# Relative bias products moved behind the sums of the first norm, in the place of its filler products

## The chip, the cores and the metric

The program runs on one core of a Trainium2 chip. A core has engines that work side by side, each through its own list of instructions in order: TensorE (PE, matrix products; its weight loads are shown as PEld), VectorE (DVE), ScalarE (ACT), GpSimd (POOL) and SyncE (SP, which here only starts transfers). They wait for each other through semaphores. The metric is the device time of one execution in microseconds (us); less is better. Before the change it is 2672.57 us, the median of three runs (2672.18 to 2675.38).

## The reference, cut to what matters

The program is four layers of transformer-like blocks on 512 tokens with 1024 features. The first thing that it computes, and the only one whose order changes, is the modulated norm ahead of the first mixer:

```python
def rms_norm(x, gain):
    xf = x.astype(jnp.float32)
    y = xf * lax.rsqrt(jnp.mean(xf * xf, axis=-1, keepdims=True) + EPS)
    return (y * gain.astype(jnp.float32)).astype(x.dtype)

def modulation(c, w, b):
    return jnp.split(jax.nn.silu(c) @ w + b, 3, axis=-1)

def sandwich(x, mod, g_pre, g_post, fn):
    shift, scale, gate = mod
    h = rms_norm(x, g_pre) * (1.0 + scale[:, None]) + shift[:, None]
    return x + gate[:, None] * rms_norm(fn(h), g_post)
```

The products that are moved have nothing to do with that norm. They prepare the attention of the second layer, several hundred microseconds later: a table of biases by distance, one row for each of 24 heads.

```python
    bias = bias_table[t5_bucket(jnp.maximum(dist, 0) * dil)].astype(jnp.float32).transpose(2, 0, 1)
    ...
    s = jnp.einsum('brnqhe,brnkhe->brnhqk', qs, kk) + bias
```

## The kernel before, in words

Features lie on the 128 partitions in 8 chunks (`x[:, c, :]`, 128 by 512 tokens). Weights come in units of 1 MB through a buffer of two slots (`raw`); ACT copies a unit into a rounded high part `whi` (`split`), POOL subtracts to get the low part `wlo`, and each product of a layer is three matmuls (high by high, low by high, high by low; lines 774 to 776). The order on every engine is written out by hand: each engine has a program of its own, which calls helpers one after the other.

The start of the program is this, with the names that the change touches:

- SP starts the transfers of `vecs`, `cst`, `x`, the first weight unit, eight units of modulation weights (`adw_a`, `adw_b`), the second weight unit and more. ACT starts those of `onehot` and `relb`.
- `bias_rows` (PE, line 1289): for each of three groups one product of `relb` (33 rows, 8 columns) with 384 columns of `onehot`, into the first three banks `LB[0]` to `LB[2]`.
- `write_bias` (ACT, line 2250): copies the three banks to `biasr`, and starts three transfers (line 2254) of 12 KB to a scratch tensor in memory, which the second layer reads back. `biasr` lies in the same memory as `hhi`, the output of the first norm. So nothing of `hhi` may be written until these transfers have landed (semaphore `scr_out`, 48 for all three).
- `load_root` (ACT, line 1953): loads the table of the square root, and `squares` (line 1933) squares the 8 chunks of `x`. PE sums each over the partitions (`feature_sum`, line 898).
- `keep_busy(3, LB[3])` (PE, line 906): three products of 128 by 128 with 256 columns, whose result nobody reads.
- `root` (ACT, line 1950) takes the square root of the sums, DVE the reciprocal (line 2711), and `root_rows` (PE, line 923) spreads it over the partitions.
- `first_rows(p)` (PE, line 1023) multiplies the modulation weights of two chunks, ACT copies them out (line 1999), `first_columns(p)` (PE, line 1031) turns them into columns, DVE makes scale and shift (lines 2840 to 2844) and scales two chunks of `x` (line 2720), ACT writes `hhi` (line 2012), DVE `hlo` (line 2750), and then PE can do the first layer's products for these chunks. This goes round four times, for p from 0 to 3.

A matmul on 4-byte floats is two instructions on PE in the trace, so the three products of `bias_rows` are six there.

Of the kernel before, what the change touches and what calls it, by code (L numbers as in the profile page):

```python
# [44 lines left out]
BIAS_PITCH = 384  # L45
# [156 lines left out]
def program(nc, a, out, stop):  # L202

    with ExitStack() as ctx:
        base = [(nc.sbuf_base + 63) // 64 * 64]

        def sb(name, shape, dt=F32, at=None):

            size = int(np.prod(shape[1:])) * 4
            off = base[0] if at is None else at  # L210
            if at is None:
                base[0] = (off + size + 31) // 32 * 32
            return nc.alloc_sbuf_tensor_at(name, shape, dt, offset=off)
# [45 lines left out]
        def vec(name, i=0, n=1):  # L259
            at, _ = VEC[name]  # L260
            return vecs[:, at + i:at + i + n]
# [40 lines left out]
        onehot = sb("onehot", [P, 3 * BIAS_PITCH], F32, h_at)  # L302
        relb = sb("relb", [P, 24], F32, h_at + 4608)
# [62 lines left out]
        s = Semaphores()  # L366
# [153 lines left out]
        LB = [ctx.enter_context(nc.psum_tensor(f"lin{i}", [P, T], F32)) for i in range(4)]  # L520
# [46 lines left out]
        for _, kc, nc_ in PLAN:  # L567
            offs.append(offs[-1] + P * kc * nc_)
# [108 lines left out]
        def _(pool):  # L677
# [64 lines left out]
            if stop > 4:  # L742
                hy_out = [kind for kind, _, _ in plan].index("hy_out")
                lows(0, hy_out + 1)
                gated_inputs()
                recurrent_branch()
                lows(hy_out + 1, len(plan))
            else:
                lows(0, len(plan))
# [3 lines left out]
        def _(pe):  # L753
# [72 lines left out]
            def lin(units, xs, chunks=None, after=None, held=None, there=0):  # L826

                _, kc, w = plan[st.u]
                first = None if chunks is None else (chunks, n.at(chunks) - there)
                for j in range(units):  # L830
                    fm_unit(st.u % 2, st.tile, kc, w // P, xs, first if j == 0 else None,
                            None if after is None else (lambda t, j=j: after(j * (w // P) + t)), None,
                            held if j == 0 else None)
                    st.u += 1
                    st.tile += w // P
                if chunks is not None:
                    n.up(chunks, kc - there)
# [64 lines left out]
            def keep_busy(rounds, bank=None):  # L902

                spare_bank = LB[(st.tile + 2) % 4] if bank is None else bank
                for _ in range(rounds):
                    pe.matmul(spare_bank[:, 0:2 * P], ident, cst[:, 0:2 * P], start=True, stop=True)

            def feature_sum(k):

                pe.wait_ge(s.sq_ok, n.up(s.sq_ok))  # L910
                chunk_sums(B4, sq[:, k % 2, :], k == 0, k == DC - 1).then_inc(s.ss_mm, 1)
# [15 lines left out]
            def root_rows(after=0):  # L927

                keep_busy(1 if after else 0)
                pe.wait_ge(s.rr_ok, n.up(s.rr_ok))  # L930
                spread_rows(B7, r_rows[:, :]).then_inc(s.rr_mm, 1)
                keep_busy(after)
# [80 lines left out]
            def first_rows(p):  # L1013

                bank = B4 if p else B5
                if p > 1:
                    pe.wait_ge(s.nb_ok, 2 * p - 1)
                for half in range(2):
                    k = FIRST_ADA[2 * p + half]
                    pe.wait_ge(ada_first_in[k], 16)  # L1020
                    for c in range(DC):
                        b = 32 * (c % 4)
                        mm = pe.matmul(bank[b:b + 32, 256 * half:256 * half + 256], silu_c[:, c:c + 1].broadcast_to([P, 32]),
                                       ada_first[k][:, c * 256:(c + 1) * 256], start=(c < 4), stop=(c >= 4))
                    mm.then_inc(s.rows_mm, 1)

            def first_columns(p):

                pe.wait_ge(s.ada_acc, n.up(s.ada_acc))
                for i in range(4):  # L1030
                    mm = pe.matmul((B4 if p else B5)[:, i:i + 1], tmp[:, p % 2, i * P:(i + 1) * P], one_per_row,
                                   start=True, stop=True)
                mm.then_inc(s.ada_mm, 1)

            def first_sums():

                for c in range(DC):
                    feature_sum(c)
                keep_busy(3, LB[3])
                root_rows()  # L1040
                first_rows(0)
                first_columns(0)

            def hgrn_mixer():
# [236 lines left out]
                    sums_after(t)  # L1281
                lin(3, hidden, None, lambda t: sums_after(t + 2))
                root_rows(2)

            def bias_rows():

                pe.wait_ge(s.extra_in, 32)
                for g in range(3):
                    pe.matmul(LB[g][0:8, 0:BIAS_PITCH], relb[0:33, 8 * g:8 * g + 8],
                              onehot[0:33, g * BIAS_PITCH:(g + 1) * BIAS_PITCH], start=True, stop=True)\  # L1290
                        .then_inc(s.bias_mm, 1)

            def attention(steps, banks, S, PT, before, between, group=1, fill=None):

# [572 lines left out]

            pe.wait_ge(s.ready, 1)
            pe.wait_ge(s.ones_in, 16)
            bias_rows()  # L1870
            pe.wait_ge(s.silu_ok, 1)
            first_sums()
            pe.wait_ge(s.bias_ok, 3)
            hgrn_mixer()
# [18 lines left out]
        def _(act):  # L1893
# [3 lines left out]
            def split(slot, size):  # L1897

                act.wait_ge(s_raw[slot], n.up(s_raw[slot], 16))
                act.activation(whi[:, slot, 0:size], raw[:, slot, 0:size], ACT.Copy).then_inc(s.whi_ok, 1)  # L1900
# [51 lines left out]
            def load_root():  # L1952
                act.activation(spare, eps_rms, ACT.Sqrt)
# [41 lines left out]
            def first_norm():  # L1995

                def rows_out(p):
                    act.wait_ge(s.rows_mm, 2 * p + 2)
                    act.activation(tmp[:, p % 2, :], (B4 if p else B5)[:, :], ACT.Copy).then_inc(s.ada_acc, 1)

                rows_out(0)
                for p in range(4):
                    shifted_chunk(0, 2 * p)
                    shifted_chunk(0, 2 * p + 1)
                    if p < 3:
                        rows_out(p + 1)
                    if p == 2:
                        split(1, UNIT)

            def shifted_chunk(ls, c):  # L2010
                    act.wait_ge(s.nb_ok, n.up(s.nb_ok))
                    act.activation(hhi[:, c, :], (B5, B6)[c % 2][:, :], ACT.Identity, bias=mods[:, ls, c:c + 1])\
                        .then_inc(s.hi_ok, 1)
# [232 lines left out]
            def write_bias():  # L2246

                for g in range(3):
                    act.wait_ge(s.bias_mm, g + 1)
                    act.activation(biasr[0:8, g, :], LB[g][0:8, 0:BIAS_PITCH], ACT.Copy, scale=BIAS_SCALE)\  # L2250
                        .then_inc(s.bias_ok, 1)
                act.wait_ge(s.bias_ok, 3)
                for g in range(3):
                    act.dma_start(scratch.ap()[g], biasr[0:8, g, :]).then_inc(s.scr_out, 16)
# [409 lines left out]
            act.wait_ge(s.c_in, 16)  # L2664
            act.wait_ge(s.ready, 1)
            act.activation(silu_c, vec("c", 0, 8), ACT.Silu).then_inc(s.silu_ok, 1)
            write_bias()
            load_root()
            act.wait_ge(s.x_in, 16)
            squares(lambda c: x[:, c, :])  # L2670
            root(1.0 / D, eps_rms)
            split(0, UNIT)
            act.wait_ge(s.scr_out, 48)
            first_norm()
            hgrn_mixer()
            if stop > 1:
# [1058 lines left out]
```

## Time and profile before

| | |
|---|---|
| median of 3 runs | 2672.57 us (2672.18 to 2675.38) |
| the profiled execution's own time | 2679.25 us |
| its span, first to last instruction | 2677.5 us |
| PE busy | 2619.9 us, 98% of the span |
| DVE, ACT, POOL busy | 44%, 36%, 36% |
| mean granted clock of TensorE | 0.994 |

All times in rows are in microseconds from the start of the span, if not marked ns. A row of the timeline has the start, the time until the last instruction of the row ends, the engine, the line of the kernel, the operation, what it writes and reads, the shape and the number of instructions; in brackets, how long the engine was idle ahead of it and what it waited for. A row of windows has the busy time of each engine in one stretch, and the granted clock of TensorE (1.00 is 2.4 GHz, 0.50 is 1.2 GHz). The first change of the granted clock that this trace holds is at 20.7 us; in stretches before that the column reads 1.00 without a record behind it.

### The profile page before, as it was taken

Reading aid. Unit: us, or ns where it says so; the run is one execution under the profiler, and the core shown is the slowest. Engines: PE = TensorE matmul, PEld = TensorE weight load, DVE = VectorE, ACT = ScalarE, POOL = GpSimd, SP = SyncE. Lnnn points to the kernel's source line nnn. Section 1 sums busy time; section 2 is a strip of 40 time slices with the busy share of each in tenths; the row PEclk is TensorE's granted clock in tenths of the full one; section 3 lists DMA queues with packets and bytes.
Section 4 is the critical chain, followed back from the end, with each engine's and each line's share of the span. In section 5 each row is a group of like instructions: output and inputs, shape, how many; then the busy total and the mean of one; then the engine's idle time right before and its main releaser. Section 6 shows DMA issues by size and latency. Waiting matters only on the chain.

```text
span 2677.5 us, 36238 instructions
## 1 busy us (share of the span) xinstructions
PE 2619.9 (98%) x14164; PEld 2116.0 (79%) x14164; DVE 1186.8 (44%) x1984; ACT 968.3 (36%) x1399; POOL 961.7 (36%) x257
## 2 busy tenths in 40 slices
PE   8999999999999999999999999999998999999998
PEld 6887787888777777888877678888877778888887
DVE  4566543343523235101258853715424565361542
ACT  4354522212533334222244843212234774321222
POOL 2222343444232223444333734444442213444442
PEclk9999999999999999999999999999999999999999
DMA  8532244542222212232222022222321112222221
GB/s 323 190 135 82 107 159 148 196 166 101 90 71 71 71 64 79 86 102 94 84 91 93 17 87 94 94 94 97 105 88 53 44 48 71 98 104 96 94 94 63
DMA packets 44032, 270.93 MB, mean 101 GB/s; under 512 B 4943, under 2 KB 8679, under 8 KB 15752
## 3 DMA queue, kind: packets, MB, share of 16 engines
q1 hardware_dynamic: 39888, 265.71, 28.2%
q10 hardware_dynamic: 4024, 3.54, 0.6%
q8 instruction: 86, 1.41, 0.2%
q14 instruction: 34, 0.28, 0.0%
HBM read 267.09 MB, written 2.13 MB: 101 GB/s over the span
## 4 chain that ended last, share of the span: by engine, by line
PE 70%; issue 22%; POOL 5%; DVE 2%; ACT 1%; POOLq 0%; ACTq 0%; DVEq 0%
PE lin L774 20%; PE lin L776 20%; PE lin L775 20%; POOL wlo L691 5%; PE lin L1322 2%; PE bank L1306 1%; PE bank L1340 1%; PE bank L1487 1%; PE bank L923 0%; PE lin L1326 0%; PE bank L1479 0%; PE lin L1479 0%; PE bank L1720 0%; PE bank L898 0%; DVE lr L3389 0%
## 5 line engine op out<-in xcount | busy, mean ns | idle before, releaser
L691 POOL TENSOR_TENSOR wlo<-raw,whi 128x2048 fp32r<-128x2048 f32 (+3 forms) x212 | 918.2, 4331 | 1671.3 <-ACT whi L1900 1671.3
L774 PE MATMUL lin<-hhi,whi 128*128 128x512 f32 x1960 | 778.2, 397 | 9.5 <-POOL wlo L691 3.6
L776 PE MATMUL lin<-hhi,wlo 128*128 128x512 f32 x1960 | 766.1, 391 | 0.0
L775 PE MATMUL lin<-hlo,whi 128*128 128x512 f32 x1960 | 765.7, 391 | 0.0
L1900 ACT ACTIVATE whi<-raw 128x2048 fp32r<-128x2048 f32 (+3 forms) x212 | 383.2, 1807 | 930.8 <-PE lin L776 863.6
L774 PEld LDWEIGHTS lin<-hhi,whi 128*128 128x128 f32 x1960 | 369.4, 188 | 102.0 <-issue 15.2
L774 PE MATMUL lin<-ghi,whi 128*128 128x512 f32 x1136 | 446.3, 393 | 3.6 <-POOL wlo L691 2.8
L776 PE MATMUL lin<-ghi,wlo 128*128 128x512 f32 x1136 | 442.8, 390 | 0.0
L775 PE MATMUL lin<-glo,whi 128*128 128x512 f32 x1136 | 442.5, 390 | 0.0
L776 PEld LDWEIGHTS lin<-hhi,wlo 128*128 128x128 f32 x1960 | 369.4, 188 | 78.4
L775 PEld LDWEIGHTS lin<-hlo,whi 128*128 128x128 f32 x1960 | 369.7, 189 | 75.4 <-issue 1.4
L774 PEld LDWEIGHTS lin<-ghi,whi 128*128 128x128 f32 x1136 | 213.7, 188 | 49.2 <-issue 4.8
L776 PEld LDWEIGHTS lin<-ghi,wlo 128*128 128x128 f32 x1136 | 213.5, 188 | 44.6
L775 PEld LDWEIGHTS lin<-glo,whi 128*128 128x128 f32 x1136 | 213.7, 188 | 43.9 <-issue 0.2
L3485 DVE TENSOR_TENSOR sq<-tmp 128x512 f32<-128x512 f32 x64 | 174.1, 2721 | 112.1 <-ACT tmp L2644 112.1
L3042 DVE TENSOR_TENSOR sq<-tmp,lin 128x512 f32<-128x512 f32 x40 | 27.5, 687 | 338.9 <-PE lin L776 320.6
L2048 ACT ACTIVATE tmp<-lin 128x512 f32<-128x512 f32 x40 | 23.9, 598 | 155.3 <-PE lin L776 155.3
L2644 ACT ACTIVATE tmp<-lin 128x512 f32<-128x512 f32 x64 | 37.6, 588 | 98.7 <-PE lin L776 98.7
L2825 DVE SCALAR_TENSOR_TENSOR bank<-adw_a,small,bank 128x256 f32<-128x256 f32 x144 | 70.5, 490 | 5.1
L3496 DVE TENSOR_TENSOR m<-m,lin 128x512 f32<-128x512 f32 x16 | 11.0, 687 | 137.2 <-PE lin L776 137.2
L3135 DVE TENSOR_REDUCE small<-lin 128x1 f32<-128x128 f32 (+3 forms) x96 | 46.7, 487 | 46.5 <-PE lin L1326 45.6
L3275 DVE TENSOR_TENSOR m<-m,lin 128x512 f32<-128x512 f32 x16 | 11.0, 687 | 118.7 <-PE lin L776 118.7
(476 smaller groups left out, 2734.1 us busy)
## 6 DMA issues: line engine op xcount, KB each, us to landing
raw<-in_w SPq DMA_DIRECT2D x171, 1024.0 KB, 4.9
adw_a<-in_ada SPq DMA_DIRECT2D x30, 1024.0 KB, 5.1
adw_b<-in_ada SPq DMA_DIRECT2D x18, 1024.0 KB, 6.8
raw<-in_w SPq DMA_DIRECT2D x20, 768.0 KB, 4.2
raw<-in_w SPq DMA_DIRECT2D x16, 640.0 KB, 3.9
raw<-in_w SPq DMA_DIRECT2D x5, 512.0 KB, 3.5
x<-in_x SPq DMA_DIRECT2D x1, 2048.0 KB, 9.9
out<-x SPq DMA_DIRECT2D x8, 256.0 KB, 2.1
```

The lines of the kernel that those rows point to most:

```text
L691: nc.gpsimd.tensor_tensor(wlo[:, slot, 0:size], raw[:, slot, 0:size], whi[:, slot, 0:size].bitcast(F32), ALU.subtract).then_inc(s.wlo_ok, 1)
L774: pe.matmul(dst, lh, rh, start=first, stop=False)
L775: pe.matmul(dst, lh, rl, start=False, stop=False)
L776: return pe.matmul(dst, ll, rh, start=False, stop=last)
L1306: pe.matmul(bank[0:64, at], p.pick[b], PT[(u - 1) % 4][:, b, :], start=(b == 0), stop=(b == q.j))
L1322: pe.matmul(bank[:, 0:q.w], q.q, q.k, start=True, stop=False)
L1900: act.activation(whi[:, slot, 0:size], raw[:, slot, 0:size], ACT.Copy).then_inc(s.whi_ok, 1)
L2644: act.activation(tmp[:, t, :], LB[(t0 + 2 * j + t) % 4][:, :], ACT.Relu).then_inc(s.ev_a, 1)
L2825: ins = v.scalar_tensor_tensor(acc[:, k % 2, :] if last else b, slot[:, c * 256:c * 256 + 256], silu_c[:, c:c + 1], b, ALU.mult, ALU.add)
L3042: v.tensor_tensor(sq[:, j, :], tmp[:, j, :], LB[(t0 + 2 * j + 1) % 4][:, :], ALU.mult)\
L3135: ins = v.tensor_reduce(top, banks[i % len(banks)][:, 0:q.w], AX_X, ALU.max, negate=True)
L3485: v.tensor_tensor(sq[:, t % 2, :], tmp[:, t % 2, :], tmp[:, t % 2, :], ALU.mult)\
```

## The change

Three edits. On PE, `bias_rows` no longer stands at the very start; it stands behind the sums of the first norm, where the three filler products were, and those are gone. On ACT, `write_bias` (three copies and three starts of transfers) moves from ahead of `load_root` to behind the split of the first weight unit. The wait for `scr_out` moves with it: it stood ahead of `first_norm`, and now stands inside it, behind the copy of the first modulation rows and ahead of the first write of `hhi`.

```diff
             def first_sums():

                 for c in range(DC):
                     feature_sum(c)
-                keep_busy(3, LB[3])
+                bias_rows()
                 root_rows()
                 first_rows(0)
                 first_columns(0)
...
             pe.wait_ge(s.ready, 1)
             pe.wait_ge(s.ones_in, 16)
-            bias_rows()
             pe.wait_ge(s.silu_ok, 1)
             first_sums()
             pe.wait_ge(s.bias_ok, 3)
...
                 rows_out(0)
+                act.wait_ge(s.scr_out, 48)
                 for p in range(4):
                     shifted_chunk(0, 2 * p)
                     shifted_chunk(0, 2 * p + 1)
...
             act.activation(silu_c, vec("c", 0, 8), ACT.Silu).then_inc(s.silu_ok, 1)
-            write_bias()
             load_root()
             act.wait_ge(s.x_in, 16)
             squares(lambda c: x[:, c, :])
             root(1.0 / D, eps_rms)
             split(0, UNIT)
-            act.wait_ge(s.scr_out, 48)
+            write_bias()
             first_norm()
```

The function `bias_rows` itself is unchanged; it only stands higher in the file, so that lines between shift.

PE, the start of its program (what is marked - stood there before, what is marked + stands there now; a row is one matmul of the source, two instructions in the trace):

```order
 L752 UNCONDITIONAL_BRANCH
-L1289 MATMUL lin<-onehot,relb 8x384 x3
 L898 MATMUL bank<-sq,cst 32x128 x32
-L906 MATMUL lin<-cst 128x256 x3
+L1039 MATMUL lin<-onehot,relb 8x384 x3
 L923 MATMUL bank<-r_rows,cst 128x128 x4
 L1023 MATMUL bank<-adw_a_132,small 32x256 x8
```

The three bias products went from the head of the queue to the place between the sums (L898) and the spreading of the root (L923), and the fillers that stood there are gone.

ACT, the start of its program before, from the table load of the first activation to the first write of `hhi`:

```order
L2666 ACTIVATE small<-vecs 128x8 [waits c_in]
L2250 ACTIVATE biasr<-lin 8x384 [waits bias_mm] x3
L2254 DMA bias_rows<-biasr 8x384 [waits bias_ok]
L2254 DMA bias_rows<-biasr 8x384 x2
L1953 ACT_TABLE_LOAD
L1953 ACTIVATE small<-small 128x1
L1933 ACTIVATE sq<-x 128x512 [waits x_in]
L1933 ACTIVATE sq<-x 128x512
L1933 ACTIVATE sq<-x 128x512 [waits ss_mm] x6
L1950 ACTIVATE r_rows<-bank,small 128x128 [waits ss_mm]
L1900 ACTIVATE whi<-raw 128x2048 [waits raw0]
L1999 ACTIVATE tmp<-bank 128x512 [waits rows_mm,scr_out]
```

And the same place now, up to the first write of `hhi`:

```order
L1952 ACT_TABLE_LOAD
L1952 ACTIVATE small<-small 128x1
L1932 ACTIVATE sq<-x 128x512 [waits x_in]
L1932 ACTIVATE sq<-x 128x512
L1932 ACTIVATE sq<-x 128x512 [waits ss_mm] x6
L1949 ACTIVATE r_rows<-bank,small 128x128 [waits ss_mm]
L1899 ACTIVATE whi<-raw 128x2048 [waits raw0]
L2250 ACTIVATE biasr<-lin 8x384 [waits bias_mm] x3
L2254 DMA bias_rows<-biasr 8x384 [waits bias_ok]
L2254 DMA bias_rows<-biasr 8x384 x2
L1998 ACTIVATE tmp<-bank 128x512 [waits rows_mm]
L2012 ACTIVATE hhi<-bank,mods 128x512 [waits nb_ok,scr_out]
```

The copies and the transfer starts moved behind `whi`, and the wait for `scr_out` moved from the copy of the modulation rows to the first write of `hhi`. (L1933 and L1932 are the same line of source, and so on.)

## Rows read from the trace of the kernel before

**Rows 1.** The page, part 1: busy time, share of the span, instructions.
```profile
PE 2619.9 (98%) x14164; PEld 2116.0 (79%) x14164; DVE 1186.8 (44%) x1984; ACT 968.3 (36%) x1399; POOL 961.7 (36%) x257
```

**Rows 2.** Timeline of PE, 3 to 24 us.
```profile
4.42 4.00 PE L1289 MATMUL lin<-onehot,relb 33*8 33x384 f32 x6 [4.42 <-DMA relb<-in_relb]
12.32 1.08 PE L898 MATMUL bank<-sq,cst 128*32 128x128 f32 x16 [3.91 <-ACT sq L1933]
...
16.53 1.18 PE L898 MATMUL bank<-sq,cst 128*32 128x128 f32 x16 [0.23 <-ACT sq L1933]
17.63 2.93 PE L906 MATMUL lin<-cst 128*128 128x256 f32 x6
20.35 1.24 PE L923 MATMUL bank<-r_rows,cst 128*128 128x128 f32 x8
21.53 1.93 PE L1023 MATMUL bank<-adw_a,small 128*32 128x256 f32 x32
```

**Rows 3.** Timeline of ACT, 3 to 28 us.
```profile
8.96 0.97 ACTq L2254 DMA_DIRECT2D bias_rows<-biasr  x3
...
11.26 0.20 ACT L1953 ACTIVATE small<-small 128x1 f32<-128x1 f32 x1
11.55 1.15 ACT L1933 ACTIVATE sq<-x 128x512 f32<-128x512 f32 x2
...
18.04 1.90 ACT L1900 ACTIVATE whi<-raw 128x2048 fp32r<-128x2048 f32 x1
23.59 0.60 ACT L1999 ACTIVATE tmp<-bank 128x512 f32<-128x512 f32 x1 [3.65 <-PE bank L1023]
26.66 1.35 ACT L2012 ACTIVATE hhi<-bank,mods 128x512 fp32r<-128x512 f32 x2 [2.48 <-DVE bank L2720]
```

**Rows 4.** Timeline of DVE, 3 to 34 us.
```profile
18.17 0.95 DVE L2711 RECIPROCAL r_rows<-r_rows 128x128 f32<-128x128 f32 x1 [17.20 <-ACT r_rows L1950]
25.33 0.16 DVE L2840 TENSOR_TENSOR mods<-bank,vecs 128x2 f32<-128x2 f32 x1 [6.21 <-PE bank L1031]
```

**Rows 5.** Timeline of all engines, 0 to 70 us.
```profile
24.24 1.05 PE L1031 MATMUL bank<-small,tmp 128*128 128x1 f32 x8 [0.78 <-ACT tmp L1999]
28.19 0.39 PE L774 MATMUL lin<-whi,hhi 128*128 128x256 f32 x1 [1.04 <-DVE hlo L2750]
```

**Rows 6.** Waits of PE, 38 to 130 us: us in total, times, longest.
```profile
PE bank L1065 <- DVE glo L2895: 1.5, 1, 1.5
PE lin L774 <- DVE hlo L2750: 1.4, 1, 1.4
```

**Rows 7.** Timeline of ACT, 98.5 to 103 us.
```profile
98.91 1.91 ACT L1900 ACTIVATE whi<-raw 128x2048 fp32r<-128x2048 f32 x1 [3.42 <-PE lin L776]
```

**Rows 8.** The transfer of x: its start, and its time to landing (tile x).
```profile
1.67 0.42 SPq L580 DMA_DIRECT2D x<-in_x  x1
...
DMA to landing us min/median/max: 9.9/9.9/9.9
```

**Rows 9.** Timeline of PE: the same shapes at 281 us and at 672 us.
```profile
281.00 1.16 PE L923 MATMUL bank<-r_rows,cst 128*128 128x128 f32 x8 [0.85 <-DVE r_rows L2711]
282.00 1.03 PE L906 MATMUL lin<-cst 128*128 128x256 f32 x4
...
672.51 1.94 PE L923 MATMUL bank<-r_rows,cst 128*128 128x128 f32 x8 [0.85 <-DVE r_rows L2711]
674.24 1.91 PE L906 MATMUL lin<-cst 128*128 128x256 f32 x4
```

**Rows 10.** Windows: stretch, length, busy by engine, PEclk, DMA share, GB/s.
```profile
102.83:109.68 6.85, 6.85 (x33) 6.85 (x33) 6.43 (x13) 0.60 (x1) 2.59 (x1) 0.50 0.15 35
109.68:112.90 3.22, 3.22 (x9) 2.54 (x10) 1.95 (x4) 0.60 (x1) 0.00 (x0) 0.50 0.99 402
112.90:116.00 3.10, 3.10 (x15) 2.58 (x14) 0.00 (x0) 0.00 (x0) 0.00 (x0) 1.00 0.93 346
672.70:676.00 3.30, 3.30 (x13) 2.73 (x13) 1.48 (x3) 0.56 (x1) 2.66 (x1) 0.50 0.18 72
```

**Rows 11.** Transfers by tile and by issue: the 27 of bias_rows; a 128 KB one before 60 us.
```profile
DMA to landing us min/median/max: 2.6/3.4/6.9
...
hmask<-in_hmask SPq DMA_DIRECT2D x1, 128.0 KB, 9.1
```

More of the change, by code:

```diff
@@ L1033, in first_columns, with bias_rows @@
                 mm.then_inc(s.ada_mm, 1)
+            def bias_rows():
+                pe.wait_ge(s.extra_in, 32)
+                for g in range(3):
+                    pe.matmul(LB[g][0:8, 0:BIAS_PITCH], relb[0:33, 8 * g:8 * g + 8],
+                              onehot[0:33, g * BIAS_PITCH:(g + 1) * BIAS_PITCH], start=True, stop=True)\
+                        .then_inc(s.bias_mm, 1)
             def first_sums():
@@ L1283, in hgrn_mixer @@
                 root_rows(2)
[L1285 to L1291, printed above, removed]
             def attention(steps, banks, S, PT, before, between, group=1, fill=None):
```

## The prediction

> **What bounds the kernel now.** I read the page first: PE is busy for 98% of the span [rows 1], so a microsecond matters where it lengthens PE's list or opens a gap in it. The change touches only the first 28 us, so I then read the timelines of PE, ACT and DVE there, and last the waits of PE behind it, to see whether a delay at the start is given back.
>
> At the start PE does the bias products from 4.42 to 8.42 us, then stands for 3.91 us until ACT has the first square [rows 2]. That square starts at 11.55 [rows 3]; `x` was started at 1.67 and took 9.9 us to land, so it landed at about 11.57 [rows 8]. ACT itself was free at 11.46 (11.26 and 0.20). Both agree within 0.1 us, and the landing is the later one: the bias work on PE and ACT ahead of it is free today, and taking it away starts nothing sooner.
>
> From there on a single chain runs: the sums end at 17.7, fillers from 17.63, the spreading of the root (L923) from 20.35, the rows L1023 from 21.53 to 23.46 [rows 2], ACT's copy at 23.59 [rows 3], the columns at 24.24 [rows 5], DVE at 25.33 [rows 4], ACT's `hhi` at 26.66 [rows 3], PE's first layer products at 28.19 after a gap of 1.04 us [rows 5]. DVE has the reciprocal at 19.12 (18.17 and 0.95) [rows 4], so it's PE's own queue, the fillers, that holds L923 until 20.35.
>
> Is a delay given back later? Between 38 and 130 us PE waits twice. The first, 1.4 us, is for `hlo`, which is the same round of PE, ACT and DVE [rows 6]. The second, 1.5 us, is for DVE's `glo`; behind that stands ACT's split at 98.91, which itself waited for PE's matmul [rows 6, 7]. Neither is tied to a transfer or to an engine that runs on its own, so a delay of the first norm goes through to the end.
>
> **The clock.** The granted clock has no record before 20.7 us, so I read it from durations. Four fillers (128x256) take 1.03 us at 282 us and 1.91 us at 674 us, where the granted clock is 0.50 [rows 9, 10]. The six at 17.63 took 2.93, 0.49 each, as at the low level (1.91 / 4 = 0.48). The eight L923 take 1.16 at 281, 1.94 in the low stretch at 672 and 1.24 here. So the clock was low (1.2 GHz) during the fillers and came up to 2.4 GHz at about 20.7, as L923 began. The six bias instructions at 4.42 took 4.00 us, 0.67 each for 384 columns: 1.5 times the columns of a filler at the low level give 0.72. So they ran at the low level, and did so from the first to the last: four microseconds of them, back to back, did not bring the clock up, while 3.1 us of fillers and the start of L923 did. The bias products use 33 rows and 8 columns of the array, the fillers 128 by 128 [rows 2]. That is the only difference that I see between them besides what stood ahead (nothing, or the sums).
>
> The Trainium skill (TensorE: Matmul & The Clock Gate, section "What's actually happening") says that the default is the throttled state, and that the clock is set by how busy the PE has been recently; it makes no difference by the size of the operands. By that rule the bias products would do for the clock what the fillers do, and the trace at 4 to 8 us speaks against it. It is the first rival.
>
> **The change, part by part.**
>
> - PE, the head: six instructions less at 4.42. Worth nothing, since `x` lands at 11.57.
> - ACT, the head: three copies and three starts (0.97 us) less before the table load. Worth nothing, for the same reason. No table is loaded more often: the copies run under any.
> - PE, behind the sums: out go 2.72 us (17.63 to 20.35), in come 4.00 less the 0.16 by which an end lies behind the next start: 3.84 at the low level. Difference +1.12, and L923 starts at about 21.47. The low level is sure until 20.7; if the clock came up there, the last 0.77 us would take half, so +0.75 is the lower end.
> - L923: 1.18 today (20.35 to 21.53), of which a third was at the low level. All low it takes 1.74 (start at 672.51 to the next start at 674.24): +0.56, or 0 at the high level.
> - L1023: 1.93 at the high level, and no row of this shape at the low one. Its bounds are 0 (nothing changes) and double, 1.73 more (21.53 to the end less the 0.2 of the tail). Here L923 and L1023 are full work, so the clock should come up within it; I take 1.3 of the 1.73.
> - L1031: eight loads and columns, 1.05 us, +0 to +0.3. I take 0, the clock being up by then.
> - Sum: 1.12 + 0.56 + 1.3 = +3.0 us at the start of the columns, and the same at the first layer product, 31.2 in place of 28.19.
> - ACT, behind the split: `whi` ends at 19.94. The copies (0.48 each) follow the three products, which end at about 19.1, 20.4 and 21.7; the last copy ends at 22.2, the starts at 23.2. The next on ACT is the copy of L1023's rows, which come at 26 or later. So this is hidden behind PE, and if PE were at the high level, still (24.2).
> - The wait for `scr_out` now stands ahead of the first `hhi`, and behind it on ACT are all writes of `hhi`, on which DVE and PE wait. The transfers start at 22.2 to 23.2. Their time to landing: 2.6 to 6.9 for the 27 transfers of this tensor, and 9.1 for a larger one while the queues are full [rows 11]. I take 5, the middle of the first, since DMA is full here too: landing at 28. `hhi` would otherwise start at 26.66 + 3.0 = 29.7. Hidden, with 1.7 us to spare; at 6.9 it lands at 29.8 and costs 0.1, at 9.1 it lands at 32 and costs 2.3.
> - DVE, POOL, SP: nothing moved. SP's next loads wait for L1023 of later rounds and come 3 us later with PE.
>
> So +3.0 us. The profiled execution would go from 2679.25 (span 2677.5 and 1.75 around it) to 2682.3. That execution lies 6.7 us above the median of the runs shown, so I put the sum on the median: 2672.57 + 3.0 = 2675.6, or +0.11%.
>
> **Rivals.**
>
> 1. The bias products keep PE busy enough, and the clock comes up at 20.7 as before. Then PE is +0.75. ACT's last copy ends at 21.8, the starts at 22.8, the landing (5 us behind the last start at 22.5) is at 27.5 to 27.8, and `hhi` starts there and not at 26.66: +1.1. For it: the stretch ahead holds the sums, which the stretch at 4 us did not. Against it: 4.00 us at the low level. Time 2673.8.
> 2. Slower: the clock stays low over the whole first round. It decides if L923 and L1023, with the pause behind them for ACT's copy, are not enough. Then 1.12 + 0.56 + 1.73 + 0.3 = 3.7; the second rows (L1023 again, +1.7) lie behind the columns with 1.04 us of gap to fill, so +0.7; and the first twelve layer products (28.19 to 29.73) grow by 0.9 of themselves, +1.4. Together +5.8, 2678.4. For it: at 102.83 to 109.68 PE was busy all the time and the clock stayed at 0.50, while it came up after the wide products from 109.68 to 112.90 [rows 10]; small or load-bound work was not enough there. Against it: L1023 has 256 columns in four strips of 32, which fill the array's width.
> 3. The landing decides. If the three writes need 9.1 us behind full queues, they land at 31.6 to 32, where `hhi` stood at 26.66: +5.2 in all, 2677.8. For it: ACT waited for `scr_out` behind 13 us of other work today, so the trace shows no wait. Against it: the transfers of this tensor took 6.9 at most.
> 4. A gain further on. At 102.83 to 112.90 the clock is low because of the pause before it. All of that now lies 3 us later, and where the clock falls need not be the same. If it doesn't fall there, up to half of 6.85 us and 1.5 us of the 3.22 are gained (seven wide products at 0.43 and not 0.23): 4.9. Net -1.9, 2670.7. For it: the low stretch begins at a pause of only 1.5 us. Against it: it could as well get longer.
>
> **How the numbers follow.** Forecast 0.49 (own range 2674.4 to 2677.4, by the ends of L1023), rival 1 0.22, rival 2 0.16, rival 3 0.05, rival 4 0.08. About 0.2%, 5.3 us, is what a measurement of this kernel can tell from no change: 2667.2 and 2677.9. Slower by more than that is most of rival 2 (0.13), half of rival 3 (0.03) and the upper tail of the forecast (0.04): 0.20. Faster by more needs rival 4 together with rival 1 and some more: 0.03. The rest, 0.77, is within. The range goes from rival 4 to a little above rival 2: 2671.2 to 2679.2.
>
> **What would show it.** The squares start at 11.5 as before. L1289's products (now behind the sums) are 0.64 us apart to the last, L923 starts at 21.4 to 21.5, and takes 1.7 and not 1.2; the first granted clock of 1.00 comes at 24 or later; ACT's first `hhi` waits for DVE and not for a transfer; the first layer product is at about 31. Rival 1 shows as a clock that is up at 20.7 and a wait of ACT for `bias_rows`. The forecast is wrong if the first layer product comes before 30 or behind 33, or if the delay there is not found in the end.

## The result

The changed kernel takes 2681.11 us in the median of 18 runs (2676.5 to 2684.27), the kernel before 2675.8 in the median of 18 (2671.98 to 2681.07). The ratio is 1.0016, with a 95% interval of 1.001 to 1.0023: slower by 4.3 us, between 2.7 and 6.2 (the two medians alone are 5.3 apart). The forecast was slower by 3.0 us at 2675.6, with a range up to 2679.2. The sign and most of the size came out; the absolute time did not, and the section on the prediction says why.

### The profile after

The page, part 1 of the changed kernel (busy time, share, instructions), to be held against [rows 1]:

```profile
PE 2618.1 (98%) x14158; PEld 2113.9 (79%) x14158; DVE 1186.8 (44%) x1984; ACT 968.1 (36%) x1399; POOL 961.7 (36%) x257
```

PE is busy for 1.8 us less in a span that is 2.3 us longer (2679.8). Busy time says nothing here.

Timeline of PE in the changed kernel, the start of the program, for [rows 2, 5]:

```profile
12.28 1.08 PE L898 MATMUL bank<-sq,cst 128*32 128x128 f32 x16 [12.28 <-ACT sq L1932]
...
17.59 4.01 PE L1039 MATMUL lin<-onehot,relb 33*8 33x384 f32 x6
21.52 2.07 PE L923 MATMUL bank<-r_rows,cst 128*128 128x128 f32 x8
23.53 3.35 PE L1023 MATMUL bank<-adw_a,small 128*32 128x256 f32 x32
27.60 1.05 PE L1031 MATMUL bank<-small,tmp 128*128 128x1 f32 x8 [0.73 <-ACT tmp L1998]
...
31.61 0.39 PE L774 MATMUL lin<-whi,hhi 128*128 128x256 f32 x1 [1.10 <-DVE hlo L2749]
```

The sums run at the same times as before. L923 starts at 21.52, where it started at 20.35; it takes 2.01 until the next start (1.18 before), L1023 takes 3.35 (1.93 before), and L1031 again 1.05. So the low level lasted from the start until near the end of L1023; the clock record of this trace begins with the rise to 1.00 at 26.4, before it was 20.7. (Here and below, the moment at which the clock comes up or falls is taken from the clock record kept in the trace; ahead of its first entry the level is read from durations.) The first layer product starts at 31.61, 3.42 after the 28.19 of before.

Timeline of ACT in the changed kernel, 3 to 36 us, for [rows 3]:

```profile
5.27 0.20 ACT L1952 ACTIVATE small<-small 128x1 f32<-128x1 f32 x1
11.51 1.15 ACT L1932 ACTIVATE sq<-x 128x512 f32<-128x512 f32 x2 [6.04 <-DMA x<-in_x]
...
21.63 0.48 ACT L2250 ACTIVATE biasr<-lin 8x384 f32<-8x384 f32 x1 [0.80 <-PE lin L1039]
22.14 0.97 ACTq L2254 DMA_DIRECT2D bias_rows<-biasr  x3
26.95 0.60 ACT L1998 ACTIVATE tmp<-bank 128x512 f32<-128x512 f32 x1 [4.84 <-PE bank L1023]
30.09 1.28 ACT L2012 ACTIVATE hhi<-bank,mods 128x512 fp32r<-128x512 f32 x2 [2.54 <-DVE bank L2719]
```

ACT is ready for the squares at 5.47 now and waits 6.04 us for `x`; the squares start at 11.51, before it was 11.55. The head of the program gave nothing back. The first `hhi` waits for DVE and not for the transfers.

Waits of PE in the changed kernel, 30 to 130 us, for [rows 6]:

```profile
PE lin L774 <- DVE hlo L2749: 2.5, 2, 1.4
PE bank L1073 <- DVE glo L2894: 1.5, 1, 1.5
```

The same waits of 1.4 and 1.5 us are there (the 2.5 holds the 1.10 of above as well). None of the 3.4 us is given back by a wait that gets shorter.

Windows of the changed kernel (stretch, length, busy of PE, PEld, DVE, ACT and POOL, granted clock, DMA share, GB/s), for [rows 10]:

```profile
108.50:115.30 6.80, 6.80 (x25) 5.93 (x24) 6.26 (x13) 0.93 (x2) 0.33 (x1) 0.51 0.46 157
166.50:169.90 3.40, 3.40 (x18) 3.40 (x18) 3.08 (x7) 3.37 (x6) 3.40 (x1) 0.52 0.42 176
```

What does change is where the clock is low later on. Before, there is one stretch of 10.2 us from 102.7 and one of 3.4 from 447.4; now there is one of 6.8 us from 108.4 and one of 3.4 from 166.4, and none near 447. If the same matmuls of both traces are laid side by side, the changed one is 3.4 us behind from the first layer product to 100 us, 1.5 behind at 107, 4.3 behind from 168 to 440, and 2.3 behind from 460 to the end. Each of these steps lies at a stretch that is low in one trace and not in the other.

### The profile page after: what moved, and what is told of

Read it like the earlier page. It is cut to its first block, busy times and chain, and to the rows that moved or that the text cites. A ratio compares the mean times of both kernels' runs of the same rounds, so it can differ in the third digit from the quotient of the medians.

```text
span 2679.8 us, 36226 instructions
## 1 busy us (share of the span) xinstructions
PE 2618.1 (98%) x14158; PEld 2113.9 (79%) x14158; DVE 1186.8 (44%) x1984; ACT 968.1 (36%) x1399; POOL 961.7 (36%) x257
## 4 chain that ended last, share of the span: by engine, by line
PE 70%; issue 22%; POOL 5%; DVE 2%; ACT 1%; POOLq 0%; ACTq 0%; DVEq 0%
PE lin L774 20%; PE lin L776 20%; PE lin L775 20%; POOL wlo L691 5%; PE lin L1322 2%; PE bank L1306 1%; PE bank L1340 1%; PE bank L1487 1%; PE bank L923 0%; PE lin L1326 0%; PE bank L1479 0%; PE lin L1479 0%; PE bank L1720 0%; PE bank L898 0%; DVE lr L3388 0%
```

## The experiments

All are compared by the start of the first layer product: 28.19 before and 31.61 after the change, the squares starting at 11.3 to 11.8 in all but one. A second trace of each kernel, further down, gave 28.32 and 31.90, so a difference of some tenths says nothing. The medians come with it, and the ratios to the kernel before that ran beside them; the full time does not follow the first layer product closely, as the run without fillers shows. The kernel before ran 35 times beside the first four (2671.07 to 2680.79, median 2675.24), 23 times beside the second four (median 2677.65) and 23 times beside the last four (median 2677.86).

### Small fillers

```diff
-                keep_busy(3, LB[3])
+                for _ in range(3):
+                    pe.matmul(LB[3][0:8, 0:2 * P], relb[0:33, 0:8], onehot[0:33, 0:2 * P], start=True, stop=True)
```

> The kernel before, with its three filler products made small: 33 rows by 8 columns (the operands of the bias products) and 256 columns, so as many and as long as before. Theory (narrow products don't bring the clock up): L923 starts at 20.3 as before, but takes 1.7 to 2.1 us and not 1.2, L1023 3.0 to 3.4 and not 1.9, the first granted clock of 1.00 comes at 23 to 27, and the first layer product at 30.0 to 30.6, where it was 28.2 before and 31.6 after the change. So about 2.2 of the 3.4 us without any bias product being moved. Median 1.5 to 3 us above before. Rival (a busy queue is enough, and the 3.4 us are the length of the bias products): the clock is up at about 20.7, first layer product at 28.2, no difference in time.

Timeline of PE with small fillers:

```profile
17.72 2.73 PE L1040 MATMUL lin<-onehot,relb 33*8 33x256 f32 x6
20.38 2.07 PE L923 MATMUL bank<-r_rows,cst 128*128 128x128 f32 x8
22.38 3.60 PE L1023 MATMUL bank<-adw_a,small 128*32 128x256 f32 x32
...
30.73 0.39 PE L774 MATMUL lin<-whi,hhi 128*128 128x256 f32 x1 [1.04 <-DVE hlo L2751]
```

L923 starts when it did before, and then L923 and L1023 take 5.6 us in place of 3.1 (L1023 alone 3.60, above the 3.4 expected). The clock came up at 25.8. First layer product 30.73 (expected 30.0 to 30.6), 2.5 us late, with no bias product moved and no longer filler. Median 2680.01, ratio 1.0008 (0.9999 to 1.0016), so in the full time the loss is not clear of noise. The rival, that a busy queue is enough, is out.

### Wide fillers as long as the bias products

```diff
-                keep_busy(3, LB[3])
+                for _ in range(3):
+                    pe.matmul(LB[3][:, 0:BIAS_PITCH], ident, x[:, 0, 0:BIAS_PITCH], start=True, stop=True)
```

> The kernel before, with its three filler products 384 columns long and not 256 (full 128 by 128 products on a part of x; the result is read by nobody): as long as the three bias products, but with the full array. Theory (width is what counts): L923 starts up to 1.1 us later than before (21.0 to 21.5), at the high level, and the first layer product at 28.8 to 29.4. Median 0.5 to 1.5 us above before. Rival (the length of what stands ahead of L923 makes the loss): as the changed kernel, first layer product at 31.6, median 3 to 4 us above before.

Timeline of PE with wide fillers:

```profile
17.68 2.98 PE L1040 MATMUL lin<-x,cst 128*128 128x384 f32 x6
20.50 1.05 PE L923 MATMUL bank<-r_rows,cst 128*128 128x128 f32 x8
21.48 1.93 PE L1023 MATMUL bank<-adw_a,small 128*32 128x256 f32 x32
```

As many columns move as in the bias products, but these take 2.98 us and not 4.01, since the clock came up at 19.3 in their midst. First layer product at 28.15, better than expected (28.8 to 29.4). Median 2676.61, ratio 0.9998 (0.9989 to 1.0007). So 384 columns ahead of L923 are not what costs, as long as the clock comes up in them. These products also read `x` and not the constants; whether what they read matters was not tested.

### Only ScalarE's half

```diff
-            write_bias()
             load_root()
...
             split(0, UNIT)
-            act.wait_ge(s.scr_out, 48)
+            write_bias()
```

The wait for `scr_out` stands inside `first_norm`, as in the change.

> Only the half of the change on ScalarE: bias products at the head and fillers as before; the copies, the transfers and the wait for them where the change puts them. Theory: PE's times up to L1023 are those of before (L923 at 20.3, the rows end at 23.5); the transfers start at 21.4 to 22.4, need 5.6 us behind the last start as in the changed kernel, and land at 27.5, so that the first write of hhi starts there and not at 26.7: first layer product at 28.9 to 29.1, +0.8. Rival (the transfers are hidden here as well): 28.2, no difference. Second rival (the half on ScalarE makes the loss of 3.4): 31.6.

Timeline of this kernel, ACT and PE:

```profile
20.03 1.20 ACT L2251 ACTIVATE biasr<-lin 8x384 f32<-8x384 f32 x3
21.27 0.97 ACTq L2255 DMA_DIRECT2D bias_rows<-biasr  x3
27.42 1.27 ACT L2013 ACTIVATE hhi<-bank,mods 128x512 fp32r<-128x512 f32 x2 [3.51 <-DMA bias_rows<-biasr]
28.94 0.39 PE L774 MATMUL lin<-whi,hhi 128*128 128x256 f32 x1 [2.06 <-DVE hlo L2750]
30.56 1.70 PE L1031 MATMUL bank<-small,tmp 128*128 128x1 f32 x8
```

Window of this kernel behind the fall of the clock (stretch, length, busy of PE, PEld, DVE, ACT and POOL, granted clock, DMA share, GB/s):

```profile
30.40:33.00 2.60, 2.60 (x14) 2.60 (x14) 0.55 (x4) 0.00 (x0) 0.00 (x0) 0.50 1.02 425
```

The transfers set `hhi`: it waits for them until 27.42, 5.2 us behind the end of the last start (21.27 and 0.97). First layer product 28.94, +0.75, in the expected band. What I had not expected is the last row of the timeline: after the longer pause of PE (2.06 in place of 1.04) the clock fell at 30.3, and L1031 took 1.70 and not 0.95. A pause of 2.02 us in the next run but one left the clock up, so the length of the pause alone does not decide it. Median 2678.34, ratio 1.0005 (0.9996 to 1.0015).

### No fillers

```diff
-                keep_busy(3, LB[3])
```

> The kernel before without its three filler products behind the sums; the bias products stay at the head. Theory: L923 starts at 19.2, when the reciprocal is there, at the low level (1.7 to 2.0 us), L1023 follows at 21.1 and the clock comes up within it or behind it, so it ends at 23 to 24.5 (before 23.5). The first layer product is at 28 to 29.2: leaving the fillers out gains 1.1 at L923 and loses it again to the clock. Median 0 to 1.5 above before. Rival (fillers are only in the way): L923 and all behind it 1.1 us sooner, first layer product at 27.1, median 1 us below before.

Timeline of PE without fillers:

```profile
19.40 2.07 PE L923 MATMUL bank<-r_rows,cst 128*128 128x128 f32 x8 [1.47 <-DVE r_rows L2710]
21.41 2.55 PE L1023 MATMUL bank<-adw_a,small 128*32 128x256 f32 x32
...
28.70 0.39 PE L774 MATMUL lin<-whi,hhi 128*128 128x256 f32 x1 [1.04 <-DVE hlo L2749]
```

L923 starts 0.95 sooner and ends only 0.12 sooner, and L1023 ends 0.50 later; the clock came up at 22.7. First layer product 28.70, inside the band. Median 2679.73, ratio 1.0015 (1.0007 to 1.0024), where I had expected 0 to 1.5 us: in the full time, leaving the fillers out costs about as much as the whole change, though only 0.5 us of it is there at the first layer product. The rest arises further on. In its trace the clock is at the low level for 36.0 us in total behind its first rise, in the two traces of the kernel before for 31.9 and 25.4. Why it is low more often is open.

### Fillers put back into the changed kernel

```diff
                 for c in range(DC):
                     feature_sum(c)
+                keep_busy(3, LB[3])
                 bias_rows()
```

> The changed kernel with the three filler products put back, ahead of the bias products behind the sums: 2.6 us more work on the chain. Theory: the fillers end at 20.3, the clock comes up at 20 to 22, the bias products run partly at the high level (1.9 to 3.0 us), L923 starts at 22.2 to 23.4 and takes 1.0, L1023 1.7, first layer product at 29.8 to 31.0: sooner than in the changed kernel (31.6) though more is computed. Median 0.5 to 2 us below the changed kernel. Rival (work ahead of L923 is what costs): 2.6 us later than the changed kernel, 34.2. A second rival: the transfers of the bias rows land last and set the start of hhi.

Timeline of this kernel, PE and ACT:

```profile
17.34 2.83 PE L906 MATMUL lin<-cst 128*128 128x256 f32 x6
20.10 2.10 PE L1039 MATMUL lin<-onehot,relb 33*8 33x384 f32 x6
22.12 1.16 PE L923 MATMUL bank<-r_rows,cst 128*128 128x128 f32 x8
23.21 1.93 PE L1023 MATMUL bank<-adw_a,small 128*32 128x256 f32 x32
29.27 1.27 ACT L2013 ACTIVATE hhi<-bank,mods 128x512 fp32r<-128x512 f32 x2 [3.46 <-DMA bias_rows<-biasr]
30.80 0.39 PE L774 MATMUL lin<-whi,hhi 128*128 128x256 f32 x1 [2.02 <-DVE hlo L2750]
```

Window of this kernel behind that pause of PE, the clock staying up:

```profile
30.80:40.00 9.20, 9.20 (x93) 8.14 (x94) 4.57 (x12) 2.17 (x4) 0.00 (x0) 1.00 1.01 402
```

The bias products take 2.10 us at the high level, and L1023 ends at 25.14, 1.7 us sooner than in the changed kernel (26.88), although 2.8 us of fillers were put ahead of it; 0.25 of this is an earlier start of the squares (11.26). The second rival of its expectation holds as well: the transfers now set `hhi`. First layer product 30.80. Median 2678.93, ratio to before 1.0011 (1.0001 to 1.0021); whether it is below the changed kernel (1.001 to 1.0023) is not shown.

### Fillers at the head, ahead of the bias products

Eight fillers ahead of `bias_rows()` at the head, and one behind each of the first seven sums, in the kernel before.

> The kernel before (bias products at the head, three fillers behind the sums) with fillers added where PE stands: eight ahead of the bias products, one behind each of the first seven sums. Theory (full-width work brings the clock up and keeps it there): the clock is up between 7 and 12 us, the last three fillers end by 19.1, L923 starts at 19.2 when the reciprocal is there and takes 1.0, L1023 ends at 22.1 (before 23.5), first layer product at 26.7 to 27.0. Median 1 to 2.5 us below before, and its runs lie closer together at the start. Rival (the clock falls back during the sums, or the fillers hold up the sums): first layer product at 28 or later and no gain.

This failed, first by my placing. The timeline of ACT and PE there:

```profile
10.29 2.10 PE L1289 MATMUL lin<-onehot,relb 33*8 33x384 f32 x6
12.93 0.97 ACTq L2255 DMA_DIRECT2D bias_rows<-biasr  x3
15.34 1.13 ACT L1934 ACTIVATE sq<-x 128x512 f32<-128x512 f32 x2
```

Window of this kernel behind the bias products:

```profile
12.90:19.60 6.70, 3.50 (x24) 1.47 (x25) 0.00 (x0) 3.79 (x7) 0.00 (x0) 0.50 1.01 426
```

ACT's queue has the copies of the bias products ahead of the squares, so holding the products back to 10.29 held the squares back to 15.34, 3.8 us. Besides, the clock did not stay up: it rose at 9.4, fell again at 12.9, 0.5 us behind the end of the bias products, and came back at 19.7, so that the first sums and their fillers ran at the low level. First layer product 34.17, 6.0 us late. Median 2681.0, ratio 1.0015 (1.0005 to 1.0026). The bias work at the head is free only while it ends before `x` lands.

### High clock, bias products behind the sums

```diff
                 for c in range(DC):
                     feature_sum(c)
+                    if c < DC - 1:
+                        pe.matmul(LB[3][:, 0:P], ident, cst[:, 0:P], start=True, stop=True)
                 bias_rows()
...
             pe.wait_ge(s.ones_in, 16)
+            keep_busy(12, LB[3])
```

> The changed kernel with full-width fillers where PE stands: twelve of 256 columns at the head (nothing on ScalarE waits for them), one of 128 columns behind each of the first seven sums. So the bias products should run behind the sums at the high level. Theory: the six of them take 2.1 us (17.6 to 19.6), L923 starts at 19.6, L1023 ends at 22.5, which alone would put the first layer product at 27.3. But the three transfers start behind the split at 21.3 to 22.3 and land at 27.3 to 27.8, so the wait for them sets hhi, and the first layer product is at 28.8 to 29.4: 2.5 us sooner than in the changed kernel, and still not sooner than before (28.2). Median 1 to 3 us below the changed kernel. Rival (the clock is not what costs): 31.6 as the changed kernel.

Timeline of this kernel, PE and ACT:

```profile
18.10 2.10 PE L1039 MATMUL lin<-onehot,relb 33*8 33x384 f32 x6
20.13 1.16 PE L923 MATMUL bank<-r_rows,cst 128*128 128x128 f32 x8
21.21 1.93 PE L1023 MATMUL bank<-adw_a,small 128*32 128x256 f32 x32
28.02 1.27 ACT L2015 ACTIVATE hhi<-bank,mods 128x512 fp32r<-128x512 f32 x2 [4.21 <-DMA bias_rows<-biasr]
29.55 0.58 PE L774 MATMUL lin<-whi,hhi 128*128 128x256 f32 x1 [2.51 <-DVE hlo L2752]
```

The clock came up at 9.1, 4.8 us behind the start of the fillers at the head (4.30). With the clock up, the bias products take 2.10 and not 4.01 us, and L1023 ends at 23.1. Still the first layer product comes at 29.55, since `hhi` waits 4.21 us for the transfers, and it runs at the low level, the clock having fallen at 29.6 after PE's pause of 2.51 us. The expected band was 28.8 to 29.4; the fillers between the sums held these up by 0.5. Median 2678.04, ratio to before 0.9996 (0.9987 to 1.0005). So at this place the change has two prices: 3.4 us that are gone when the clock is up, and behind them, hidden as long as the first is paid, 0.75 us (only ScalarE's half) to 1.4 us (here) by the wait for the transfers. In the full time this run is the best evidence on the cause: the changed kernel is 1.001 to 1.0023 of the kernel before, and with the clock up at most 1.0005.

### High clock, bias products at the head

The kernel before with `keep_busy(4, LB[3])` behind `bias_rows()` at the head and the same 128-column product behind each of the first seven sums.

> The kernel before with full-width fillers where PE stands: four of 256 columns behind the bias products at the head, one of 128 columns behind each of the first seven sums; the three behind the last sum stay. ScalarE's order and waits are those of before. Theory: the clock is up between 12 and 16 us, the squares still start at 11.5, the last three fillers take 1.3 and not 2.7 us, L923 starts at 19.2 when the reciprocal is there, L1023 ends at 22.1, first layer product at 26.8 to 27.3 (before 28.2): the version that beats both, by 1 to 1.5 us against before and 4 to 5 against the changed kernel. Rival: while the clock is still low the fillers hold up the sums, the squares wait, and L923 comes at 20 or later, with no gain.

Timeline of PE in this kernel:

```profile
18.74 1.56 PE L906 MATMUL lin<-cst 128*128 128x256 f32 x6
20.29 1.16 PE L923 MATMUL bank<-r_rows,cst 128*128 128x128 f32 x8
21.38 1.93 PE L1023 MATMUL bank<-adw_a,small 128*32 128x256 f32 x32
...
28.04 0.39 PE L774 MATMUL lin<-whi,hhi 128*128 128x256 f32 x1 [0.35 <-DVE hlo L2753]
```

The last three fillers take 1.56 and not 2.93, but they start 1.1 us later (18.74), because the fillers between the sums hold these up: the rival of its expectation. First layer product 28.04. Median 2675.27, ratio to before 0.9996 (0.9987 to 1.0004). By the ratios it beats the changed kernel (1.001 at least), and it is not shown to beat the one before. Here the clock came up at 13.6. PE had then been at work since 4.47 with one gap of 0.31 us, but on wide fillers only since 8.39, 5.2 us before. That is about as long as in the two runs with the fillers first (4.8 and 5.5 us), as if the bias products ahead had not counted.

### Rows or columns

The kernel before, its three fillers with 256 moving columns, as 128 rows by 8 columns in one run and as 33 rows by 128 columns in the other. One run of each, so that only the traces are used and not the times.

> The kernel before with its three fillers as 128 rows by 8 columns, 256 columns moving. It tells rows from columns: if few output columns are what keeps the clock low, L923 takes 1.9 to 2.1 and L1023 3 or more, as in the run with 33 by 8, and the first layer product is at 30 to 31. If few rows are, it is at 28.2 as before. I expect the columns to count, and so 30 to 31.

> The kernel before with its three fillers as 33 rows by 128 columns, 256 columns moving. If few rows keep the clock low, first layer product at 30 to 31; if only few columns do, 28.2 as before. I expect 28.2 to 28.6, less surely than for the run with 128 by 8.

Timeline of PE, first with 128 by 8:

```profile
17.53 2.75 PE L1040 MATMUL lin<-cst 128*8 128x256 f32 x6
20.21 1.16 PE L923 MATMUL bank<-r_rows,cst 128*128 128x128 f32 x8
21.30 1.93 PE L1023 MATMUL bank<-adw_a,small 128*32 128x256 f32 x32
```

and with 33 by 128:

```profile
17.69 2.93 PE L1040 MATMUL lin<-cst 33*128 33x256 f32 x6
20.54 2.08 PE L923 MATMUL bank<-r_rows,cst 128*128 128x128 f32 x8
22.55 3.31 PE L1023 MATMUL bank<-adw_a,small 128*32 128x256 f32 x32
```

Both of my guesses were wrong. With all rows and 8 columns the clock is up at 20.1 and the first layer product comes at 27.96, as before; with 33 rows and all columns the clock is up at 25.4 and it comes at 30.59, as with the small fillers (30.73). Among these shapes it's the rows. That rests on one trace each, but the clock comes up at moments that are over 5 us apart, and in two traces of one and the same kernel they are 0.4 us (before) and 1.0 us (changed) apart.

### Both kernels once more

> The kernel before, once more, for a second trace. Theory: the point at which the clock comes up differs from execution to execution (20.7 in the first trace), and with it L923 and L1023: first layer product between 28 and 30 after a start of the squares at 11.5. Rival: the same 28.2 to 0.1 us.

> The changed kernel, once more, for a second trace. Theory: the clock comes up at a different point between 23 and 27 or even later, first layer product between 30.4 and 32 or, if the clock is not up by the end of L1023, 32 to 34. Rival: 31.6 to 0.1 us.

The kernel before: clock up at 21.1, L923 in 1.47, first layer product 28.32; 2676.58 us. The changed kernel: clock up at 27.4, behind the end of L1023, L1023 in 3.64, first layer product 31.90; 2679.68 us. So the difference at this place is 3.42 in the first pair of traces and 3.58 in the second. The spread between executions is smaller than I had expected here, and it isn't where the times differ: the two traces of the kernel before are 0.1 us apart at the wait at 102.8 us (102.83 and 102.93) and 2.7 us apart at the end (spans of 2677.5 and 2674.8). The second of them has no low stretch at 672 us and a shorter one at the end (3.6 for 6.6 us). The second pair, laid side by side, differs from the first: the changed kernel is 3.6 us behind until 100 us, 1.3 ahead from 115 to 130, 1.1 behind from 200 to 440, level from 460 to 670 and 3.1 behind at the end.

## Why the prediction was right or wrong

**The absolute time: wrong, and by the reference.** The step that failed is "I put the sum on the median". I had noted that the profiled execution (2679.25) lay 6.7 us above the median of three and took the three for the better guide. Over 18 runs, of which these three are the first, the median before is 2675.8; over 35 others it is 2675.24, and over 23 and 23 more 2677.65 and 2677.86. So the three were 2.7 to 5.3 us too low. On 2675.8 the same sum gives 2678.8. Of the 5.5 us between forecast and result, 3.2 are this reference; the other 2.3 (5.3 between the medians for 3.0) are size, 0.4 to 0.6 of them at the first layer product and the rest further on, where its cause is open. The sum on the profiled execution, 2682.3, would have been nearer, but that is luck as well: it was one execution out of such a spread. The three did not show how wide the runs lie; 35 of them range over 9.7 us, and follow the mean granted clock that each run lists: the 8 with a clock of 0.997 average 2672.1, the 9 with 0.994 average 2679.1. My range came from the mechanisms alone and held nothing for that. It had two slips besides: the ends of L1023 (0 and 1.73) give 2674.3 to 2676.0 and not 2674.4 to 2677.4, and the lower end, 2671.2, leaves out rival 4 at 2670.7. And I took 5.3 us as what can be told from no change; the interval of the result is 1.8 us to either side.

**What bounds it: right.** Squares at 11.51 and 11.55; the head was free, and failed to be only when the bias products were held back beyond the landing of `x` (the run with fillers at the head).

**Bias products in the place of the fillers, +1.12: right** (+1.17, 21.52 for 20.35).

**L923, +0.56: too small.** Measured +0.83 (2.01 for 1.18). I took the row at 672 us, where L923 began 0.17 us before the clock fell (672.68), so 0.17 of the 0.27 us that are missing can lie there. Twice the start-to-start time of the row at 281 us (281.00 to 282.00) would have given 2.0.

**L1023, +1.3 of 1.73: right** (+1.42; in the second trace of the changed kernel +1.71, all of it at the low level). **L1031, 0: right** (1.05 in both).

**Sum at the first layer product, +3.0: measured +3.42 and +3.58**, of which the small fillers alone give 2.5. The rest up to the 4.3 of the ratio is within its interval (2.7 to 6.2), and what the low stretches further on do with it I can't predict: in the two pairs that were laid side by side the distance went from 3.4 and 3.6 to 2.3 and 3.1 at the end, by way of 4.3 behind and 1.3 ahead.

**The clock: right, for half of the reason, and in part by luck.** The bias products behind the sums don't bring the clock up; I had named the array's use as the only difference that I saw, and argued with rows and columns together. Of the shapes tried, it is the rows that decide. But my argument from the head was worth nothing: four microseconds of bias products did not bring the clock up there, and wide fillers from the head on didn't either in that time, they took 4.8 and 5.5 us.

**The wait for the transfers: right.** Landing expected at 28, with `hhi` at 29.7; measured, `hhi` at 30.09 and waiting for DVE. The 5 us taken for it were close to what the runs in which it decides show (5.2 to 5.6). It is a real wait where PE is quicker (the half on ScalarE, the fillers put back, the high clock).

**Rival 1** (busy is enough) is refuted by the small fillers. By the Trainium skill (TensorE: Matmul & The Clock Gate, section "What's actually happening") the clock is set by how busy the PE has been recently, and the section makes no difference by the operands. The traces don't agree with that as it stands: the kernel before and the run with small fillers have the same queue, and differ by 2.5 us. **Rival 2** (low through the first round) did not happen in either trace of the changed kernel, though in the second the clock came up only behind L1023. **Rival 3** did not decide. **Rival 4** is half there: in the first trace the low stretch at 103 us got shorter by 3.4 us, and another came at 166.4; in the second there is none near 103 at all, and three others came, at 164, 1376 and 1505. I had put that stretch down to PE's pause of 1.5 us. The second trace has the same pause (1.45) and the clock stays up, so the pause alone is not the cause, and what decides is open.

## What to carry to other kernels

Products that nobody reads can be what keeps the rest fast: before replacing them with useful work, look at how many of the array's rows that work uses (33 did not do here, 128 did), and not only at how long it keeps the queue full. Read the clock from the duration of the same shape elsewhere, since the column of the granted clock can be empty at the start. Judge the mechanism of a change of some microseconds at one place of the trace, and its worth by many runs: through the clock further on, 0.5 us at that place was 4 us in the full time without the fillers. Three runs don't give the time of such a kernel.

## What the runs showed of the hardware

- Behind the sums, 2.7 to 2.9 us of matmuls with 33 active rows (8 or 128 columns) left the clock at the low level, with L923 in 2.1 us behind them and the rise at 25.8 and 25.4; the same with 128 active rows and only 8 columns had it up at 20.1 (L923 in 1.16). One trace of each. The bias products, 4.0 us with 33 rows and 8 columns, left it low in both traces of the changed kernel.
- From a start at the low level, wide fillers at the head had the clock up 4.8 us (4.30 to 9.1), 5.5 us (3.96 to 9.4) and, behind 4.0 us of bias products, 5.2 us (8.39 to 13.6) after the first of them.
- A pause of PE of 2.06 us (only ScalarE's half) was followed by a fall of the clock at 30.3, and one of 2.51 us (high clock) by one at 29.6; in the first L1031 then took 1.70 and not 0.95. One of 2.02 us (fillers put back) left the clock up until 105.3. So a wait can cost more than its length, and its length does not tell whether it will.
- Three writes of 12 KB to memory needed 5.2 us (from 22.24, the end of the last start, to 27.42), 5.5 us (22.51 to 28.02) and 5.6 us (23.72 to 29.27) until ScalarE went on, with the DMA engines' share at 1.00 to 1.02 in these stretches.
